# Linear attention rescheduled between weight blocks, in a kernel of two transformer blocks on Trainium2

## The reference

```python
q, k, v, r, glr = split(h @ w_in)        # 4 heads, 128 for q and k, 256 for v and r
log_a = log_sigmoid(glr @ w_gate + b_gate) / 16
# within a chunk: b = cumsum(log_a); S is the state of a head, 128 x 256
o_inter = (q * exp(b)) @ S
attn[i, j] = sum_k q[i, k] * k[j, k] * exp(b[i, k] - b[j, k])      # j <= i
o = o_inter + attn @ v
S = S * exp(b_last) + (k * exp(b_last - b)).T @ v
y = (rmsnorm(o, g_out) * silu(r)) @ w_out
```

## Time and profile before

| | |
|---|---|
| runs before | 3167.91, 3167.92, 3170.71 us; median 3167.92 |
| the profiled execution's own time | 3173.78 us |
| its span, first to last instruction | 3171.7 us |
| TensorE busy | 3067.8 us, 97% |
| VectorE, ScalarE, GpSimd busy | 1595.6 (50%), 1150.7 (36%), 1755.0 us (55%) |
| mean granted TensorE clock | 0.988 |
| end of layer 0's projection in the trace | 321.2 us |

### The profile page before, as it was taken

One profiled execution on the slowest core, in us unless ns is written; L12 is line 12 of the kernel. 1 busy time (PEld: TensorE's weight loads), 2 busy tenths in 40 slices (PEclk: granted clock), 3 DMA queues, 4 the chain that ended last, 5 costly groups with the idle time before them and its releaser, 6 DMA issues.

```text
span 3171.7 us, 44168 instructions
## 1 busy us (share of the span) xinstructions
PE 3067.8 (97%) x14616; PEld 2495.4 (79%) x14616; DVE 1595.6 (50%) x2794; ACT 1150.7 (36%) x1478; POOL 1755.0 (55%) x2024
## 2 busy tenths in 40 slices
PE   7988999999999999988999999999999999999998
PEld 4777788877678888766788888888888888888887
DVE  6863555322545541994309997444411444454443
ACT  4354322236532222423333234555543332233232
POOL 1723677645057765773446665444445666666663
PEclk8999999999999999999999999999999999999999
DMA  8511455422045553221224445555564655556652
GB/s 338 184 46 54 158 190 189 155 77 92 21 135 190 190 182 101 88 93 54 87 87 134 145 132 180 189 195 182 177 241 141 225 195 192 180 181 204 205 193 78
DMA packets 170201, 481.94 MB, mean 152 GB/s; under 512 B 15360, under 2 KB 48896, under 8 KB 168080
## 3 DMA queue, kind: packets, MB, share of 16 engines
q1 hardware_dynamic: 147680, 410.83, 39.3%
q10 hardware_dynamic: 22448, 70.14, 5.6%
HBM read 411.70 MB, written 69.21 MB: 152 GB/s over the span
## 4 chain that ended last, share of the span: by engine, by line
PE 56%; issue 20%; POOL 18%; DVE 3%; ACT 1%; DMA 0%; DVEq 0%; POOLq 0%; SPq 0%; ACTq 0%
PE ps L1672 52%; POOL w_lo L552 18%; PE pa L1672 4%; DVE s_acc L1451 1%; DMA e_g<-expert_act 0%; DVEq L1448 0%; DVE s_tmp L1517 0%; DVE mg_lo L1519 0%; ACT mg_hi L923 0%; DVE s_m L1515 0%; DVE x L1127 0%; DVE s_gl L1439 0%; ACT L620 0%; POOLq L550 0%; POOLq L556 0%
## 5 line engine op out<-in xcount | busy, mean ns | idle before, releaser
L552 POOL TENSOR_TENSOR w_lo<-raw,w_hi 128x256 fp32r<-128x256 f32 x2020 | 1754.8, 900 | 1387.3 <-ACT w_hi L570 1385.8
L1672 PE MATMUL ps<-h_hi,w_hi 128*128 128x512 f32 x2392 | 946.4, 396 | 24.1 <-POOL w_lo L552 11.3
L1672 PE MATMUL ps<-h_hi,w_lo 128*128 128x512 f32 x2392 | 936.7, 392 | 0.0
L1672 PE MATMUL ps<-h_lo,w_hi 128*128 128x512 f32 x2392 | 912.4, 390 | 0.0
L570 ACT ACTIVATE w_hi<-raw 128x1024 fp32r<-128x1024 f32 x509 | 538.8, 1060 | 808.2 <-PE ps L1672 687.1
L1672 PEld LDWEIGHTS ps<-h_hi,w_hi 128*128 128x128 f32 x2392 | 451.9, 189 | 126.0 <-issue 18.3
L1672 PEld LDWEIGHTS ps<-h_hi,w_lo 128*128 128x128 f32 x2392 | 451.7, 189 | 95.8
L1672 PEld LDWEIGHTS ps<-h_lo,w_hi 128*128 128x128 f32 x2392 | 451.6, 189 | 92.9 <-issue 1.0
L1672 PE MATMUL ps<-wa_hi,w_hi 128*128 128x512 f32 x1024 | 398.5, 389 | 1.3 <-DVE x L1636 1.3
L1672 PE MATMUL ps<-wa_hi,w_lo 128*128 128x512 f32 x1024 | 398.4, 389 | 0.0
L1672 PE MATMUL ps<-wa_lo,w_hi 128*128 128x512 f32 x1024 | 398.4, 389 | 0.0
(11 more groups left out here) (322 smaller groups left out, 3072.7 us busy)
## 6 DMA issues: line engine op xcount, KB each, us to landing
ada<-in_ada SPq DMA_DIRECT2D x144, 512.0 KB, 4.4
raw<-in_expert_u SPq DMA_DIRECT2D x128, 512.0 KB, 4.1
raw<-in_expert_v SPq DMA_DIRECT2D x128, 512.0 KB, 4.1
raw<-in_ffn_in SPq DMA_DIRECT2D x88, 512.0 KB, 3.5
expert_act<-g_act ACTq DMA_DIRECT2D x128, 256.0 KB, 4.2
gate_matrix<-w_st ACTq DMA_DIRECT2D x16, 2048.0 KB, 6.7
e_w<-gate_matrix SPq DMA_DIRECT2D x16, 2048.0 KB, 11.3
e_g<-expert_act SPq DMA_DIRECT2D x128, 256.0 KB, 7.7
```

The lines of the kernel that those rows point to most:

```text
L552: last = nc.gpsimd.tensor_tensor(w_lo[:, k, c:c + 256], raw[:, k, c:c + 256], w_hi[:, k, c:c + 256].bitcast(F32), ALU.subtract)
L1672: return nc.tensor.matmul(out, a, b, start=start, stop=stop_)
```

## The change

It has four parts, all in layer 0.

- **Loads and start.** x is loaded ahead of the first four weight blocks, which now alternate with modulation blocks; ScalarE squares four tiles of x, then alternates a conversion with a square; VectorE alternates products, w_lo and h tiles; w_lo of block 4 moves from GpSimd to VectorE; TensorE's last step finishes the first four tiles one after another. ScalarE converts one block further ahead (`t + 4`).
- **Items.** They begin after the first v block, by the table `ITEMS_BY`; 14 blocks carry them. Two banks of `pa` turn, and an item is kept two items later. Modulation products 16 to 23 come earlier, 24 to 31 one per item, 32 to 47 beside the output projection, loaded once og_ready has reached 8.
- **State.** Keys are decayed, transposed and multiplied with v chunk by chunk between blocks, in the two free banks of `pa`, and the three states are kept in three buffers. Queries are scaled head by head.
- **Output.** Output products go head by head over all four chunks into `pa` and are squared and gated straight from there; the last two r blocks, the sums of squares and the heads alternate, and each head passes its norm, h_hi and h_lo by itself.

The core of the diff; "..." marks what is left out.

```diff
         for n in range(2 * DT):
             sp_ada0(sp, n)
             if n == 1:
-                for m in range(RING):
-                    sp_raw(sp, m, A["gla_qk"][m - 1, :, :] if m else A["gla_glr"][:, :], 1024)
                 sp.dma_start(x[:, :, :], A["x"].rearrange("k p t -> p k t")).then_inc(ld_x, 16)
+            if 1 <= n <= RING:
+                m = n - 1
+                sp_raw(sp, m, A["gla_qk"][m - 1, :, :] if m else A["gla_glr"][:, :], 1024)
         for m in range(RING, 8):
             sp_raw(sp, m, A["gla_qk"][m - 1, :, :], 1024)
         for j in range(16, 24):
             sp_ada0(sp, j)
         sp_raw(sp, 8, A["gla_qk"][7, :, :], 1024)
         for m in range(8):
-            if m < 6:
+            if m < 2:
                 for j in range(24 + 4 * m, 28 + 4 * m):
                     sp_ada0(sp, j)
             sp_raw(sp, M0["gla_v"] + m, A["gla_v"][m, :, :], 1024)
-        for name in ("gla_r", "gla_out"):
-            sp_segment(sp, name, A[name], 1024)
+        sp_segment(sp, "gla_r", A["gla_r"], 1024)
+        for k in range(8):
+            if k == 4:
+                sp.wait_ge(og_ready, DT)
+                for j in range(32, 40):
+                    sp_ada0(sp, j)
+            if k >= 5:
+                for j in range(40 + 4 * (k - 5), min(48, 44 + 4 * (k - 5))):
+                    sp_ada0(sp, j)
+            sp_raw(sp, M0["gla_out"] + k, A["gla_out"][k, :, :], 1024)
...
+        pool.wait_ge(lo_done, RING + 1)
+        for m in range(RING + 1, 2 * RING):
+            split(m, m % RING)
+        with pool.Fori(2, last // RING) as i:
...
+    def act_first(act, hi):
+
+        def square(k):
+            if k >= 4:
+                act.wait_ge(sq0_mm, k - 3)
+            nc.scalar.activation(nsq[:, k % 4, :], x[:, k, :], ACT.Square).then_inc(sq_ready, 1)
+
+        act.wait_ge(ld_x, 16)
+        for k in range(4):
+            square(k)
+        for m in range(RING):
+            hi.upto(m)
+            square(4 + m)
+        nc.scalar.preload_act_table_set(LN_EXP)
+        act.wait_ge(sq0_mm, DT)
+        own_a.link(act, nc.scalar.activation(rstd[:, :], pa[:, 0, :], ACT.Ln, scale=1.0 / D, bias=EPS))
+        nc.scalar.activation(rstd[:, :], rstd[:, :], ACT.Exp, scale=-0.5).then_inc(rs_ready, 1)
+        for k in range(DT):
+            act_h_tile(act, 0, k)
...
-    def items_by(b):
-
-        return 0 if b < 3 else min(ITEMS, (b - 2) * 2)
+    BLOCKS = 14
+    ITEMS_BY = (1, 3, 5, 8, 10, 13, 15, 18, 20, 23, 26, 29, 32, 32)
+    KEY_D = (2, 7, 13)
+    KEY_MM, STATE_MM = (3, 5, 7), (8, 10, 12)
+    STATE_AT = (22, 27, 31)
+    EB_AT, QE_AT = (8, 9, 10, 12), (20, 25, 29, 32)
+    R_CHUNKS = BLOCKS - 8
+
+    def o_stats(h):
+
+        return (ps[:, (T0["gla_out"] + h) % RING, :] if h < 2 else pa[:, 2 * (h - 2), :])
 
     Z_AT = RING
-    R_ITEMS, R_CHUNKS = 4, 6
...
+                if taken[0] - 2 in KEY_D:
+                    c = KEY_D.index(taken[0] - 2)
+                    act.wait_ge(ke_d, c + 1)
+                    nc.scalar.activation(g_ke[:, :, :], g_ke[:, :, :], ACT.Exp, scale=1.0 / TAU).then_inc(ke_e, 1)
...
-        for b in range(8 + R_ITEMS):
+        for b in range(BLOCKS):
             m, T = M0["gla_v"] + b, T0["gla_v"] + b
             hi.upto(m + 3)
-            levels(items_by(b) + 1)
+            if b - 1 in KEY_MM:
+                c = KEY_MM.index(b - 1)
+                act.wait_ge(kt_mm, c + 1)
+                nc.scalar.activation(g_kT[c][:, :, :], pa[:, 2, :].rearrange("p (h k) -> p h k", h=GH), ACT.Copy)\
+                  .then_inc(kt_out, 1)
+            levels(ITEMS_BY[b] + 1)
+            for h in range(GH):
+                if b == EB_AT[h]:
+                    act.wait_ge(ke_d, TT - 1)
+                    nc.scalar.activation(g_b[:, h, :], g_b[:, h, :], ACT.Exp, scale=1.0 / TAU).then_inc(eb_done, 1)
             if b == 3:
-                act.wait_ge(ada_done, 48)
+                act.wait_ge(ada_done, 28)
...
+        for q in range(4):
+            square(q)
+            if q % 2 == 1:
+                r_gate(R_CHUNKS + q // 2)
+        hi.upto(M0["gla_out"] + 3)
+        nc.scalar.preload_act_table_set(LN_EXP)
+        rms(0)
+        square(4)
+        square(5)
+        rms(1)
+        head_hi(0)
+        square(6)
+        square(7)
+        rms(2)
+        head_hi(1)
+        rms(3)
+        head_hi(2)
+        head_hi(3)
...
+        ada_product(0, 0)
+        ada_product(0, 1)
+        dve.wait_ge(ld_c, 32)
+        first_gain(0)
+        block_lo(0)
+        ada_product(1, 0)
+        block_lo(1)
+        ada_product(1, 1)
+        block_lo(2)
+        first_gain(1)
+        ada_product(2, 0)
+        block_lo(3)
+        dve.wait_ge(rs_ready, 1)
+        dve_scale(0, 0)
+        ada_product(2, 1)
+        dve_scale(0, 1)
+        dve_lo(dve, 0, 0)
+        first_gain(2)
+        for k in range(3, DT):
+            ada_product(k, 0)
+            dve_scale(0, k - 1)
+            ada_product(k, 1)
+            dve_lo(dve, 0, k - 2)
+            first_gain(k)
+        dve_lo(dve, 0, DT - 2)
+        dve_scale(0, DT - 1)
+        dve_lo(dve, 0, DT - 1)
+        block_lo(RING)
...
+            if n in KEY_D:
+                key_decay(KEY_D.index(n))
+            if n - 2 in KEY_D:
+                key_scaled(KEY_D.index(n - 2))
+            if n in STATE_AT:
+                state(STATE_AT.index(n))
+            if n in QE_AT:
+                query_scaled(QE_AT.index(n))
             h, l, e = item_level(n)
             if l < LEVELS:
                 if e + 1 < GH * LEVELS:
                     gate_sums(e + 1)
                 scaled(n)
-            if n:
-                keep(n - 1)
+            if n >= 2:
+                keep(n - 2)
+            if 1 <= n <= 8:
+                adas(23 + n, 24 + n)
+        keep(ITEMS - 2)
...
+        gated(0)
+        gated(1)
+        normed(0)
+        gated(2)
+        head_lo(0)
+        normed(1)
+        gated(3)
+        head_lo(1)
+        normed(2)
+        head_lo(2)
+        normed(3)
+        head_lo(3)
+
+        m, T = M0["gla_out"], T0["gla_out"]
+        dve.wait_ge(tile_free, T)
+        j = 32
         for k in range(DT):
-            if k == 0:
-                dve.wait_ge(r_silu, 1)
-            if k >= R_CHUNKS:
-                dve.wait_ge(tile_free, T0["gla_r"] + k + 1)
-            dve.wait_ge(oq_ready, k + 1)
-            nc.vector.scalar_tensor_tensor(out=g_o[:, k, :], in0=g_o[:, k, :], scalar=col("gla_g_out", k % 2),
-                                           in1=g_r[:, k, :], op0=ALU.mult, op1=ALU.mult).then_inc(og_ready, 1)
-        dve.wait_ge(ors_ready, 1)
-        for k in range(DT):
-            dve.wait_ge(og_ready, k + 1)
-            nc.vector.tensor_tensor(g_o[:, k, :], g_o[:, k, :], g_rs[:, k // 2, :], ALU.mult).then_inc(ot_ready, 1)
-        for k in range(DT):
-            dve.wait_ge(oh_hi, k + 1)
-            nc.vector.tensor_tensor(h_lo[:, k, :], g_o[:, k, :], h_hi[:, k, :].bitcast(F32), ALU.subtract).then_inc(o_ready, 1)
-        dve.wait_ge(ld_x, 16)
-        dve_residual(dve, "gla_out", 1, 0, 1)
+            dve_squares(dve, 1, k - 1)
+            n = (6, 2, 2, 2, 2, 2, 0, 0)[k]
+            adas(j, j + n)
+            j += n
+            if k == 6:
+                dve_mod(dve, 24, 24, 48, [(1, "norm_ffn0")])
...
+        for k in range(DT - 1):
+            pe.wait_ge(hh_ready, k + 1)
+            for t in range(RING):
+                h_part(t, k)
+            if k:
+                pe.wait_ge(h_ready, k)
+                for t in range(RING):
+                    l_part(t, k - 1)
+        pe.wait_ge(hh_ready, DT)
+        pe.wait_ge(h_ready, DT)
+        for t in range(RING):
+            h_part(t, DT - 1)
+            l_part(t, DT - 2)
+            l_part(t, DT - 1).then_inc(blk_done, 1)
...
-                if a >= 4:
-                    pe.wait_ge(lv_cp, a - 3)
+                if a >= 2:
+                    pe.wait_ge(lv_cp, a - 1)
...
-        for b in range(8 + R_ITEMS):
+        for b in range(BLOCKS):
...
-            items(items_by(b))
-        items(ITEMS)
-        for b in range(R_ITEMS, R_CHUNKS):
-            r_tile(b)
-
-        pe.wait_ge(tile_free, T0["gla_r"] + R_CHUNKS)
-        pe.wait_ge(lv_cp, ITEMS)
-        pe.wait_ge(qe_ready, 2)
-        for c in range(TT):
-            w = slice(c * GCH, (c + 1) * GCH)
-            if c < TT - 1:
-                if c >= 2:
-                    pe.wait_ge(kt_out, c - 1)
-                for h in range(GH):
-                    last = nc.tensor.transpose(ps[:, 2 + c % 2, h * P:(h + 1) * P], g_k[:, h, w], ident)
-                last.then_inc(kt_mm, 1)
-            if c >= 2:
-                pe.wait_ge(o_out, 2 * (c - 1))
-            if c:
-                pe.wait_ge(st_out, c)
-            for h in range(GH):
-                for a in range(2):
-                    out = pa[:, 2 * (c % 2) + a, h * GCH:(h + 1) * GCH]
-                    d = slice(a * P, (a + 1) * P)
```

(64 more changed lines are left out.)

254 lines of the change are left out of this document (131 added, 123 removed).

## The result

The changed kernel takes 3130.33 us (median of four runs, 3127.95 to 3132.52) against 3167.91 for the kernel before beside it (3167.12 to 3170.71): ratio 0.9877, 95% interval 0.9865 to 0.9889, so 37.6 us less. The forecast was 3130. The profiled execution took 3127.95 us, 45.8 less than the profiled one of before; how that differs from 37.6 comes further down.

The account below looks back on a forecast made before the run. TensorE was taken as the bound of the changed layer; 0.8 - 5.9 - 10.2 - 23.0 = -38.3 us gave 3135.5 from the profiled 3173.8, or 3130 against the median 3167.9. Range 3118 to 3148.

Parts of the forecast that it names:

- part 1: Start, up to the end of the first four tiles: no gain from the new order, +0.8 us, bounds -2 and +4.
- part 2: Gap before tile 4: VectorE has block 4's w_lo ready at 58.8, before it is needed at 59.1; -5.9 us.
- part 3: Value and gate blocks: items go with every block and VectorE keeps up; 124.7 to 114.5 us, -10.2.
- part 4: Output, norm and projection: state chain gone, TensorE's work plus 1.5 us of hand-overs is 74.9 of 97.9 us; -23.0.
- SyncE's queue: Rival: sixteen modulation loads go one at a time ahead of projection blocks 4 to 7; 60 us slower, 3228, chance 0.04.
- part 5: Clock during and after the gate product: the drop to 0.50 stays; 0, with a gain of at most 3.3 us.
- VectorE as the bound of part 3: Rival: VectorE limits the value and gate blocks; 7 to 10 us back, 3139, upper end 3144, chance 0.22.
- No decoupling: Rival: with two banks every item waits for the copy of the one two before; 23 us back, 3152, chance 0.06.
- The clock rival: Rival: the clock stays high through the gate product, 0.9 and 2.4 us less there; 3125, chance 0.08.

Follow-up runs that it names:

- the repeat: The changed kernel itself, unedited, run and profiled once more: 3131.34 us, ratio 0.9878; 27.1 us from the gate product's start to the first value block.
- the last version: Changed kernel with three warm-up matmul pairs instead of eight and modulation products 28 to 31 moved to items 10, 12, 14, 16: 3131.41 us, ratio 0.9874.

## Why the prediction was right, point by point

**The whole.** 3130.3 against 3130. The layer gave 41.0 us for 38.3 in the profiled executions. Inside that, 4.1 us more than forecast before the value blocks (3.2 of it the clock) stand against 1.5 less in them. With the repeat's z to v, 1.6 us longer, 41.0 would have been 39.4. The sum, its stages and what fills them held; that the median came within 1 us is luck as well, since against the clock of its own profile the forecast was 3135.5 and the profiled execution took 3127.95.

**The start (part 1).** Forecast 0.8 us later, measured 0.1 sooner: the four tiles end at 58.2. A step that failed is rstd: I had it done at 28.4 us with the squares queueing behind the warm-ups, and it was done at 27.86. They did queue, 3.04 us of wait in ScalarE's timeline, but Ln began at 26.60, before it was 26.84:

```profile
20.26 0.63 ACT L664 ACTIVATE nsq<-x 128x512 f32<-128x512 f32 x1 [3.04 <-PE pa L1798]
...
26.60 0.60 ACT L674 ACTIVATE rstd<-pa 128x512 f32<-128x512 f32 x1
```

The last h_lo was done at 54.5 for my 55.4, and the sixteen matmuls behind it took 3.7 us for my 3.6. That VectorE's work sets the end holds for the new order alone. Before, VectorE had its last h_lo at 50.9 us, and the products that it made from there on, which I counted in its 27.35 of 27.9, were not needed for these tiles; TensorE had the longer list then. That a change of order gives nothing came out right, but by a reading of the earlier trace rows that was not.

**The gap before tile 4 (part 2).** Forecast 5.9 less, ready at 58.8. VectorE made w_lo from 56.98 to 58.2 and no wait is left; the gate product began 5.94 us sooner, 0.1 of it from the start. Undone alone it costs 5.0 up to there.

**Value and gate blocks (part 3).** 116.0 us for 114.5. The waits were 2.7 us (0.53, 0.85, 0.69, 0.60) for my 3, two of the four in places that I had named (items 9 and 31, not 28); the others are at item 0 and at item 7, the first diagonal, whose short chain I had not walked. What was mis-sized is TensorE's work, 113.3 for 111.5. I had taken 5.44 us for a block from a run of blocks. After a burst of items a block takes 5.54 to 5.56 us in each of the thirteen cases (181.01 to 186.55 us is one), as its first two products start 0.31 to 0.32 apart instead of 0.23; that is 1.3 of the 1.8 us. VectorE was busy 90.3 us of 116.0 for my 98. In that sum the item's passes were mixed: the key pass had 0.79 and 0.41 in the earlier trace rows and 0.61 on average now, from this group of DVE between 89.5 and 205.4 us:

```profile
L1304 DVE TENSOR_TENSOR g_kq<-g_k,g_E 128x256 f32<-128x256 f32 x28 | 17.2, 614 | 0.5 <-ACT g_E L735 0.5
```

VectorE was full in the beginning, 22.0 of 22.0 us from 98 to 120, and had 21 of its spare 26 us after 140. GpSimd was busy 54.6 us of this stage. The Trainium skill (GPSIMD Engine Reference, 1. Specifications) has the two engines contend where VectorE has two inputs from SBUF; the 0.61, between 0.41 alone and 0.79 beside GpSimd, goes that way.

**Output, norm, projection (part 4).** 74.8 us for 74.9. Where did the 23.1 come from? The stage of before had 12.6 us of waits (1.93 and 2.83 in the earlier trace rows, and 1.41, 2.12, 1.02, 1.40 and 1.84 before them in its timeline), now 0.4; state products and their transposes, 7.0 us of work, moved among the blocks. The remaining 3.9 are near the low clock of the earlier trace rows: 5% of 31.6 us and 11% of 15.9 are 3.3. By the runs, the state chain alone is 4.8, the order of the heads' norm 1.4 to 2.2, the place of the gate blocks 0: some 7 of the 12.2 us. That squares and gates now read the outputs straight from `pa`, without a copy to g_o first, was not undone by itself, and what it carries is not shown. SyncE's queue took no part: the sixteen loads took 8.2 us to land in the median, about the 7.9 of the rival, but they went beside one another, all transfers at 411 GB/s together between 240 and 260 us, and the only wait of the projection was 0.16 us for w_lo. DMA issues from 205 to 281 us and windows of the kernel after:

```profile
ada<-in_ada SPq DMA_DIRECT2D x16, 512.0 KB, 8.2
```

```profile
240.00:260.00 20.00, 20.00 (x90) 16.57 (x89) 18.51 (x29) 5.15 (x7) 6.10 (x8) 1.00 1.02 411
260.00:281.00 21.00, 20.23 (x89) 16.09 (x88) 18.17 (x24) 7.39 (x9) 17.76 (x18) 1.00 0.47 178
```

**The clock (part 5).** I said that the drop stays, as the same instructions stand there. In this profile it did not: z to v is 25.5 us, before it was 28.7, 3.2 less, and my bound was 3.3. The step that failed is to take it as a property of the instructions. It changes from one execution of the same program to the next, and a forecast for a median would have to take a middle value. The Trainium skill (TensorE: Matmul & The Clock Gate, Part 1) has the clock fall after idling, which foretells 1.00 here. This profile agrees, but it is no vindication of the rule: in the repeat the clock fell with TensorE busy throughout.

**The rivals.** VectorE as the bound of part 3: no, but the early stretch is at its limit, and one more pass per item shows it. No decoupling: no, and 14 us is what the later copy prevents, nearer to my 23 than to nothing. SyncE's queue: no. The clock rival's event did happen in the profiled execution and gave its 3.2 us there, but not in all executions, and the median is 3130 and not its 3125.

**What stays open.** What decides whether and how soon after the gate product's start the clock falls: the table and the distances are read off, not tested. What two banks of `pa` cost against four, and what the outputs without a copy bring: no run has them alone. And the 1.8 us of the last version: shown in one trace each, not in the medians.
